# Opening of a two-layer trunk in two parts of features: 768 columns of the first modulation pieces, then x and two weights, then the other 256

## The reference

```python
c_act = jax.nn.silu(c)                                    # (1, 1024)
mod = (c_act @ w_ada[l] + b_ada[l])[:, None, :]           # six vectors of 1024
sh1, sc1, gt1, sh2, sc2, gt2 = jnp.split(mod, 6, axis=-1)
h = x * (1.0 + sc1) + sh1
proj = h @ w_in                                           # 9 groups of columns: q, k, v of two head groups, indexer
# rope on the q's and k's; sliding-window attention with sinks; indexer picks 128 keys of 512
# per query; RMS norms; output projection; layer norm; then mod2, SwiGLU, layer norm
```

## Time and profile before

| | |
|---|---|
| median of 3 runs | 1275.48 us (1275.37 to 1276.41) |
| profiled execution, whole run | 1276.25 us |
| its span | 1274.6 us |
| TensorE matmul busy | 1235.8 us, 97% |
| VectorE, ScalarE, GpSimd busy | 801.5, 510.5, 274.2 us |
| granted TensorE clock | 0.998 of full speed |
| first real product | at 33.01 us of the span |

### The profile page before, as it was taken

One profiled execution on the slowest core, in us unless ns is written; L12 is line 12 of the kernel. 1 busy time (PEld: TensorE's weight loads), 2 busy tenths in 40 slices (PEclk: granted clock), 3 DMA queues, 4 the chain that ended last, 5 costly groups with the idle time before them and its releaser, 6 DMA issues. The chain is left out here.

```text
span 1274.6 us, 18347 instructions
## 1 busy us (share of the span) xinstructions
PE 1235.8 (97%) x6394; PEld 1031.6 (81%) x6394; DVE 801.5 (63%) x1400; ACT 510.5 (40%) x1027; POOL 274.2 (22%) x281
## 2 busy tenths in 40 slices
PE   6999989999999999999999999999999999999997
PEld 5778876889888888888888688778988888888886
DVE  6889997677777764333676699856733355433338
ACT  3555568345232212222145466862643321222220
POOL 4027236600111010000007367570000000000000
PEclk9999999999999999999999999999999999999999
DMA  9672012334878554222523120112232223332211
GB/s 358 240 270 79 33 51 67 132 116 150 279 264 270 193 168 175 90 93 98 171 94 117 66 67 2 37 63 84 75 124 99 97 101 132 99 98 89 94 65 66
DMA packets 44850, 158.30 MB, mean 124 GB/s; under 512 B 5872, under 2 KB 5872, under 8 KB 44784
## 3 DMA queue, kind: packets, MB, share of 16 engines
q1 hardware_dynamic: 30528, 109.07, 24.8%
q0 software_dynamic: 12960, 47.19, 10.9%
q10 hardware_dynamic: 1296, 1.17, 0.3%
HBM read 155.31 MB, written 2.10 MB: 123 GB/s over the span
## 5 line engine op out<-in xcount | busy, mean ns | idle before, releaser
L631 PE MATMUL bank<-hT_hi,w_hi 128*128 128x512 f32 x640 | 249.5, 390 | 0.0
L633 PE MATMUL bank<-hT_hi,w_lo 128*128 128x512 f32 x640 | 249.0, 389 | 0.0
L632 PE MATMUL bank<-hT_lo,w_hi 128*128 128x512 f32 x640 | 249.0, 389 | 0.0
L1967 DVE TENSOR_TENSOR w_lo<-w_raw,w_hi 128x1024 fp32r<-128x1024 f32 x88 | 107.9, 1226 | 147.0 <-ACT w_hi L1434 147.0
L1280 ACT ACTIVATE w_hi<-w_raw 128x1024 fp32r<-128x1024 f32 x96 | 100.7, 1062 | 202.8 <-PE bank L633 189.0
L1434 ACT ACTIVATE w_hi<-w_raw 128x1024 fp32r<-128x1024 f32 x88 | 93.0, 1057 | 161.1 <-PE bank L633 155.8
L631 PE MATMUL bank<-w_hi,hT_hi 128*128 128x512 f32 (+2 forms) x392 | 148.1, 378 | 2.9 <-ACT pq L1316 2.0
L1544 DVE TENSOR_TENSOR w_lo<-w_raw,w_hi 128x1024 fp32r<-128x1024 f32 x88 | 114.1, 1310 | 53.6 <-ACT w_hi L1280 52.2
L633 PE MATMUL bank<-w_hi,hT_lo 128*128 128x512 f32 (+2 forms) x392 | 142.6, 364 | 0.0
L632 PE MATMUL bank<-w_lo,hT_hi 128*128 128x512 f32 (+2 forms) x392 | 142.3, 363 | 0.0
L633 PEld LDWEIGHTS bank<-hT_hi,w_lo 128*128 128x128 f32 x640 | 120.1, 188 | 25.3
(11 more groups left out here) (207 smaller groups left out, 2199.5 us busy)
## 6 DMA issues: line engine op xcount, KB each, us to landing
w_raw<-in_weights SPq DMA_DIRECT2D x184, 512.0 KB, 3.5
ada_w<-in_w_ada POOLq DMA_DIRECT2D x80, 512.0 KB, 5.2
ada_w<-in_w_ada SPq DMA_DIRECT2D x4, 512.0 KB, 6.6
qT<-in_w_ada SPq DMA_DIRECT2D x4, 512.0 KB, 10.0
xs<-in_x SPq DMA_DIRECT2D x4, 512.0 KB, 15.4
g_row<-in_ln_row POOLq DMA_DIRECT2D x4, 512.0 KB, 5.2
b_row<-in_ln_row POOLq DMA_DIRECT2D x4, 512.0 KB, 6.1
trunk_out<-xs SPq DMA_DIRECT2D x8, 256.0 KB, 2.1
```

What stands on the lines that cost most here:

```text
L631: pe.matmul(dst, a_hi, b_hi, start=first, stop=False)
L632: pe.matmul(dst, a_hi, b_lo, start=False, stop=False)
L633: return pe.matmul(dst, a_lo, b_hi, start=False, stop=last)
L1967: nc.vector.tensor_tensor(w_lo[:, s, :], w_raw[:, s, :], w_hi[:, s, :].bitcast(F32), ALU.subtract).then_inc(lo_ready, 1)
```

## The change

The first 16 modulation pieces are loaded, scaled and summed in two parts of columns: 768 (`EARLY`, six feature blocks, `KE = 6`), and later the other 256 (`LATE`). SyncE loads the early parts, then x0, w0, w1, x1, w2, x2, x3, then the 16 late parts (two semaphores for eight each), then w3. The piece 11 goes from VectorE's share to ScalarE's and GpSimd's, so that each of the four sums has four pieces; `rope_tables` runs behind VectorE's first group and not within it. Coefficients, transposes, scaling and splits exist for six blocks (`early_...`, in groups of three blocks per engine), and once more for the last two blocks of all four tiles together (`late_...`). `open_first` takes the place of `project_first` in layer 0: for each tile the products of six features, the late sums and transposes behind tile 2, and at the end the two last features for all four tiles. The dummy products are 11, 1 and 3 pairs. Layer 1 is not touched.

```diff
-SUM_FIRST = ((1, 3, 5, 7), (8, 9, 10))
-VECTOR_FIRST = ((0, 2, 4, 6), (11, 12, 13, 14, 15))
+SUM_FIRST = ((1, 3, 5, 7), (8, 9, 10, 11))
+VECTOR_FIRST = ((0, 2, 4, 6), (12, 13, 14, 15))
+KE = 6
+EARLY = KE * P
+LATE = slice(EARLY, D_MODEL)
...
             for n in range(2 * KD):
-                sp.dma_start(first_ada[n], w_ada[n // KD, n % KD]).then_inc(ada_first_in[n], 16)
+                sp.dma_start(first_ada[n][:, 0:EARLY], w_ada[n // KD, n % KD][:, 0:EARLY])\
+                    .then_inc(ada_first_in[n], 16)
...
             load_x(2)
+            load_x(3)
+            for n in range(2 * KD):
+                sp.dma_start(first_ada[n][:, LATE], w_ada[n // KD, n % KD][:, LATE])\
+                    .then_inc(ada_late_in[n // KD], 16)
             load_w(3)
-            load_x(3)
...
+            def late_mod():
+                pe.wait_ge(h_scaled_dve, scaled_dve(0, 2))
+                pe.wait_ge(h_scaled_act, at_tile(0, 2))
+                for vector in (False, True):
+                    for g in range(2):
+                        if vector:
+                            pe.wait_ge(late_sum, 4 * (g + 1))
+                        else:
+                            pe.wait_ge(ada_summed, 6 + 3 * (g + 1))
...
+            def open_first():
...
+                pe.wait_ge(h_hi, at_tile(0, 0))
+                for j in range(2):
+                    pe.wait_ge(hi_ready, converted(0, p0 + j))
+                    pairs(0, j, hT_hi, w_hi)
+                early_transpose(1)
+                pe.wait_ge(lo_ready, converted(0, p0))
+                pairs(0, 0, hT_hi, w_lo)
+                pe.wait_ge(h_lo, at_tile(0, 0))
+                for j in range(2):
+                    pairs(0, j, hT_lo, w_hi)
+                pe.wait_ge(lo_ready, converted(0, p0 + 1))
+                pairs(0, 1, hT_hi, w_lo)
+                pe.wait_ge(hi_ready, converted(0, p0 + 2))
+                pairs(0, 2, hT_hi, w_hi)
+                pairs(0, 2, hT_lo, w_hi)
+                early_transpose(2)
+                pe.wait_ge(lo_ready, converted(0, p0 + 2))
+                pairs(0, 2, hT_hi, w_lo)
+                for t in range(1, T):
+                    pe.wait_ge(h_hi, at_tile(0, t))
+                    for j in range(n - 1):
+                        pairs(t, j, hT_hi, w_hi)
+                    if t == 1:
+                        early_transpose(T - 1)
+                    pe.wait_ge(h_lo, at_tile(0, t))
+                    for j in range(n - 1):
+                        pairs(t, j, hT_lo, w_hi)
+                        m = pairs(t, j, hT_hi, w_lo)
+                        if t == T - 1:
+                            m.then_inc(piece_used, 1)
+                    if t == T - 2:
+                        late_mod()
+                        late_transpose()
+                pe.wait_ge(late_hi, 1)
+                pe.wait_ge(hi_ready, converted(0, p0 + n - 1))
+                for t in range(T):
+                    for k in range(KE, KD):
+                        product(t, k, hT_hi, w_hi)
+                    if t == 0:
+                        pe.wait_ge(lo_ready, converted(0, p0 + n - 1))
+                    for k in range(KE, KD):
+                        product(t, k, hT_hi, w_lo)
+                    if t == 0:
+                        pe.wait_ge(late_lo, 1)
+                    for k in range(KE, KD):
+                        m = product(t, k, hT_lo, w_hi, last=k == KD - 1)
+                    m.then_inc(tile_done if t < T - 1 else piece_used, 1)
...
-            keep_clock(6)
+            keep_clock(1)
             first_mod(1, False, True)
             first_mod(1, True, False)
             pe.wait_ge(rope_table, 2)
-            transpose_x(0, 0, 4)
-            pe.wait_ge(mod_taken, 2)
-            transpose_x(0, 1, 4)
+            early_transpose(0)
+            keep_clock(3)
...
             convert(0, 1)
-            build_h(0, 0, 4, 0)
+            build_early(0, 1)
             convert(0, 2)
-            for t in range(1, T):
-                build_h(0, t, 4, (None, 3, 4, 4)[t])
+            build_early(1, 3)
+            build_early(2, 3)
+            scale_late(0)
+            build_early(T - 1, 3)
+            scale_late(1)
+            convert(0, 4)
+            build_late()
...
             first_vector(0)
+            dve.wait_ge(pos_in, 16 * 2)
+            rope_tables()
             first_vector(1)
             dve.wait_ge(small_in, 16 * 4)
-            take_mod(0, 2)
+            take_early()
+            first_coefficients(0, KE, coef_ready)
+            scale_early(0)
+            convert(0, 1)
+            split_early(0)
+            convert(0, 2)
+            scale_early(1)
+            convert(0, 3)
+            split_early(1)
+            scale_early(2)
+            late_vector(0)
+            split_early(2)
+            scale_early(T - 1)
+            late_vector(1)
+            split_early(T - 1)
+            convert(0, 4)
             rope_signs()
...
+            take_late()
+            first_coefficients(KE, KD, late_coef)
+            build_late()
...
                 if l == 0:
+                    convert(l, C0P[1] + 1)
                     for t in range(2):
                         rope_direct(t)
-                    convert(l, C0P[1] + 1)
                     ada_group(2, 0, 2)
```

More of the change, by code:

```diff
@@ L205, in build_trunk @@
         ada_first_in = [sem(f"ada_first_in{i}") for i in range(2 * KD)]
+        ada_late_in = [sem(f"ada_late_in{i}") for i in range(2)]
         ada_in = [sem(f"ada_in{i}") for i in range(RING)]
@@ L282, in mod_column, with late_column @@
             return bank[b][:, at:at + n]
+        def late_column(g, k, n):
+            at = (2 * g + k - KE) * 64
+            return bank[4][:, at:at + n]
         def columns_to(g):
@@ L551, in _ @@
             summed = 0
[L552 to L560, removed]
+            for part, cols in enumerate((slice(0, EARLY), LATE)):
+                for g in range(2):
+                    first, total = SUM_FIRST[g][:2]
+                    for i, n in enumerate(SUM_FIRST[g][1:]):
+                        pool.wait_ge(ada_scaled, 8 * part + 4 * g + i + 2)
+                        if i > 0:
+                            pool.wait_ge(ada_summed, summed)
+                        nc.gpsimd.tensor_tensor(first_ada[total][:, cols], first_ada[total][:, cols],
+                                                first_ada[n if i else first][:, cols], ALU.add)\
+                            .then_inc(ada_summed, 1)
+                        summed += 1
             for l in range(DEPTH):
@@ L772, in block @@
                         m.then_inc(tile_done, 1)
[L774 to L798, removed]
-                    pe.wait_ge(lo_ready, converted(0, p0 + 2))
-                    products(2, hT_hi, w_lo)
-                for pair in range(2):
[L803 to L807, removed]
-                        transpose_x(0, T - 1, 4)
-                        for t in range(2):
-                            block(t, n - 1)
-                        continue
+                for pair in range(2):
                     for j in range(n):
@@ new lines, in take_late, with first_coefficients @@
+            def take_late():
+                dve.wait_ge(mod_reduced, 2)
+                for g in range(2):
+                    nc.vector.tensor_tensor(mod[:, g, KE:KD], bank[4][:, 128 * g:128 * (g + 1):64], modb[:, g, KE:KD],
+                                            ALU.add).then_inc(mod_taken, 1)
+                dve.wait_ge(mod_taken, 2)
+            def first_coefficients(k0, k1, ready):
+                ks = slice(k0, k1)
+                nc.vector.scalar_tensor_tensor(out=hcoef[:, 0, 0, ks], in0=mod[:, 1, ks], scalar=1.0,
+                                               in1=lnc[:, 0, 0, ks], op0=ALU.add, op1=ALU.mult)
+                step(nc.vector.scalar_tensor_tensor(out=hcoef[:, 0, 1, ks], in0=mod[:, 1, ks], scalar=1.0,
+                                                    in1=lnc[:, 0, 1, ks], op0=ALU.add, op1=ALU.mult))
+                nc.vector.tensor_tensor(hcoef[:, 0, 1, ks], hcoef[:, 0, 1, ks], mod[:, 0, ks], ALU.add)\
+                    .then_inc(ready, 1)
+                dve.wait_ge(ready, 1)
@@ new lines, in scale_early @@
+            def scale_early(t):
+                dve.wait_ge(x_transposed, at_tile(0, t))
+                parts_free(dve, 0, t)
+                for k in range(3):
+                    m = nc.vector.tensor_scalar(h_part(0, t)[:, k * P:(k + 1) * P],
+                                                bank[4 + 2 * (t % 2)][:, k * P:(k + 1) * P],
+                                                hcoef[:, 0, 0, k:k + 1], hcoef[:, 0, 1, k:k + 1], ALU.mult, ALU.add)
+                m.then_inc(h_scaled_dve, 1)
```

155 lines of the change are left out of this document (131 added, 24 removed).

## The result

The changed kernel takes 1279.28 us (median of 9 runs, 1278.62 to 1280.65), the kernel before 1275.48 (1275.29 to 1276.49): ratio 1.0029, 95% interval 1.002 to 1.0038. The change makes the kernel 3.8 us slower; 2.0 us faster was forecast. The profiled run of the changed kernel ("after" from here on) took 1278.62 us, the lowest of its nine; its span is 1276.7.

The account below looks back on a forecast made before the run. TensorE is 97% busy; the 33.0 us opening is a serial chain. Gain: 5.9 (opening) - 2.8 (work moved) + 0.6 (waits) - 1.0 (stall) - 0.5 (contention) - 0.2 (clock) = 2.0 us: 1273.5, own range 1272.6 to 1274.6, overall 1271.7 to 1276.0.

Parts of the forecast that it names:

- The failed step: VectorE in the opening: rope tables in one block behind group 0, 4.5 us, to 17.5; group 1's sums done at 21.8.
- the fourth block: TensorE's last block of column sums in the opening: from 22.6 to 24.0 us, visible at 24.2; before 29.4.
- the first product: End of the opening chain on TensorE: at 27.1 us, 5.9 us earlier than 33.01.
- contention: GpSimd's six late adds beside VectorE instructions reading two SBUF tensors: bounds 0 to 1.4 us, 0.5 taken as cost.
- Rival D: Clock falls as TensorE idles 1.1, 0.5 and 0.7 us between 26 and 32 us: costs 2.8, giving 1276.3; chance 0.05.
- The baseline: Differences taken from the profiled execution (whole run 1276.25 us) and subtracted from the median of the runs, 1275.48.
- the first projection: Stretch from 27.1 to 54.8 us (before to 58.48): 2.8 us of work moved in, waits 1.5 instead of 2.1.
- contention and clock: Two costs set aside: 0.5 us for late GpSimd adds beside VectorE, 0.2 for a clock that rises late.
- GpSimd's adds: Six adds of 768 columns in the opening, 1.83 us each from 10.2, ending at 21.2 against 24.2 before.
- TensorE's stall at piece 6: Second projection: TensorE waits 0.9 us for VectorE's low half of piece 6, with restart 1.0.
- rival C: Late columns block the in-order queues of VectorE and ScalarE; first projection ends 4.7 us later, 1278.2; chance 0.07.
- VectorE's wait of 3.55 there: VectorE's 3.55 us wait ahead of the index scores, said to be exactly the slack used up; scores reached at 86.5.

Follow-up runs that it names:

- Experiment 1: The changed kernel with the rope tables put back behind VectorE's first piece, as before the change: 1274.84 us, ratio to the kernel before 0.9994.
- experiment 2: The changed kernel with the four rope-table multiplies writing a PSUM bank and one copy bringing the angles back to SBUF: 1276.91 us, ratio 1.0006.
- experiment 5: The changed kernel with rope tables behind VectorE's first piece and five dummy pairs, not one, ahead of TensorE's third block of sums: 1275.15 us.
- experiment 7: Experiment 5 without GpSimd's six adds of the late 256 columns, so part of the modulation sums is missing: 1274.75 us.
- experiment 3: The changed kernel with six more pairs of dummy products between TensorE's third and fourth block of sums: 1277.62 us.
- experiment 11: The kernel before, unchanged, run again for a second trace: 1276.41 us.
- experiment 4: The kernel before with only the rope tables moved behind VectorE's first group: 1283.91 us, ratio 1.006.
- experiment 8: The kernel before with only piece 11 moved from VectorE's share to ScalarE's and GpSimd's, adds still 1024 columns: 1278.51 us, ratio 1.0024.

## Why the prediction was wrong

*The failed step.* "VectorE: the rope tables now run in one block behind it, 13.76 - 9.26 = 4.5 us, to 17.5." The block was measured at 8.4. I took its length from a place where its cast and multiplies were over before GpSimd began (its first add at 11.67) and moved it to one where GpSimd adds nearly without a pause. The sums end at 26.1 in place of 21.8 (3.9 by the block, 0.5 since it began at 13.49 and not at 13.0), so the fourth block starts 3.2 us later than forecast (25.80 for 22.6). With the low clock, another 1.3 were lost from there to the first product. Experiment 1 shows the cause, experiment 2 and the single instructions the kind: each waits for the end of the running add. The slowed ones read one SBUF tensor and write SBUF; the line right behind them (18.28, 0.30) reads SBUF and writes PSUM and is not slowed, nor are those of the block that read a PSUM bank beside an SBUF tensor and write SBUF (L2112, 0.49 for two, as before).

I had weighed contention, but for the late columns alone, and there the size fits (0.5 forecast; 0.5 between the traces of experiments 5 and 7, which holds the adds' own time too). The rows that I had for it say the same as the single multiplies: in the earlier trace rows the low half ends 1.08 us behind the GpSimd instruction that ran when it began (97.47 to 98.78), and the next GpSimd instruction 1.16 behind the low half. One behind the other, they need about what each needs alone (1.22 and 1.29); I read it as a slowing by 1.7. The section Specifications of "GPSIMD Engine Reference" in the Trainium skill gives two conditions for contention with VectorE, two SBUF inputs or a 2-port performance mode; I used the first and passed over the second. "VectorE: DVE Perf Modes" (Why PSUM operands drop a tier) says that a PSUM operand excludes the 2-port mode, and the runs agree: 0.71 us for four multiplies with a PSUM destination, 3.89 without.

*The clock.* Rival D had the mechanism and got 0.05. It looked for idle time between 26 and 32 us in the sound opening; the gap of 2.22 us at 23.6 was made by the failed step. It costs 0.9 to 1.7 us (experiment 3), not 2.8: the clock was low from 26.4 to 29.8 us, and not for 6 us. My argument that gaps of 1.11 and 0.22 us had not lowered the clock was worth less than it looked: the same kernel shows the fall in its other trace.

*The baseline.* I took differences from a trace of 1276.25 us and subtracted them from a median of 1275.48. That trace holds 0.85 us of a clock that rose late (experiment 11), which a run near the median need not hold. The sum of the miss: 5.8 us = 4.5 at the first product (27.1 forecast, 31.59) + 0.5 in the first projection (28.2 for 27.7) - 0.7 set aside for contention and clock + 0.1 behind the index products + 0.77 for that baseline + 0.66, by which after's trace lies below its own median.

*Right.* Loads to within 0.5 us (piece 3 at 9.4 for 9.2, w0 at 23.6 for 23.1), GpSimd's adds (1.81 each where 1.83 was forecast, the last ending at 21.96 for 21.2), scaling 1.15 and copy 0.84 (1.13 and 0.83), TensorE's stall at piece 6 (0.66 us and the restart; one projection step takes 4.52 us in place of 3.60, so 0.92; forecast 1.0), no wait of VectorE ahead of the scores. Nothing waited for late loads near 35 us: rival C did not come about. With the failed step repaired, experiment 5 reaches the first product at 27.90 and the index products at 85.91 (forecast 27.1 and 85.3).

*Right, but not priced.* "VectorE's wait of 3.55 there was exactly the slack used up." I wrote that and gave it no price. Slack used up costs nothing in a run in which everything is on time; a load 1.2 us late then costs 1.3 us (three traces), and 4 of 11 runs of experiment 5 lie that much higher. So the repaired change is worth some 0.6 us in its good runs (1274.7 against 1275.4) and less in the median, where 2.0 were forecast. Experiment 5's trace starts its index products 1.4 us ahead of the reference trace (85.91 against 87.31), but 0.85 of that is the late clock of the latter: a run of before with an early rise and no fall should start them near 86.46 (87.31 - 0.85), and the lower level of its runs wants the same (1275.4 - 1188.9 = 86.5). Against that 0.55 is won, which agrees with the 0.6 of the runs. No trace of such a run of before exists, so this is worked out, not shown.

## What to carry to other kernels

A block that is moved takes a new duration from its new neighbours: before pricing it, look at what runs on GpSimd beside the new place. A VectorE cast or multiply by a scalar from SBUF to SBUF that meets a running GpSimd add is to be priced at the rest of that add; of a row of short ones two got through per add here. For the multiplies a PSUM destination avoided it. An engine's wait ahead of a shared point is the reserve for late loads, not waste: a change that uses it up should be charged with the scatter of the loads. Dummy products that hold the clock take twice as long until it rises, so they can themselves be what the next step waits for. Two traces of the kernel before, and the list of its runs with their clocks, help to tell which level the reference trace is of.

## What the hardware showed that I had not expected

- Four 128x32 multiplies, SBUF to SBUF, beside GpSimd's adds: 3.89 us (adds of 1.83) and 4.96 us (adds of 2.36), against 0.68 to 0.71 alone or with a PSUM destination; a cast of 128x4 0.82 and 1.01 against 0.17. In the traces of after and of experiments 3 and 4 each slow one ends 0.02 to 0.04 us behind the end of a GpSimd add, the others take 0.23 to 0.24. GpSimd's adds hardly suffered (1.81 to 1.85 each beside them, 1.81 without).
- Idle times of TensorE of 2.22, 1.83, 1.70 and 1.37 us, the last in the unchanged kernel, were each followed by a granted clock of 0.50 (1.2 GHz). It is not the same in every run: experiment 8's trace idles 1.52 us at 25.2 and 1.87 us at 32.3 and keeps 1.00; by the mean clock, experiment 1 had the fall in 2 of 11 runs, after in all nine. What decides between them stays open.
- The same 22 dummy products, begun at 10.47 us, took 7.12 us in one trace and 7.99 in another: the clock rises at a time that differs from run to run, and the first product differed with it by 0.9 us.
